# A one-layer hybrid decoder step: tokens in five tiles of 108 to 110 rows at both ends, the gate product on four row groups, the last block divided at 328 tokens

## What is computed

```python
xn = rmsnorm(x, norm_mix_g)
proj = xn @ w_in + b_in            # all branches' inputs and the gates
lg = log_sigmoid(ga @ w_gla_a2 + b_gla_a2) / 16      # ga: 16 columns of proj
...                                # three branches o_b: GLA, mLSTM, RG-LRU
x = x + (sum_b sigmoid(gates_b) * (o_b @ w_branch_b)) @ w_out
u = causal_dwconv(rmsnorm(x, norm_ffn_g) @ w_up)
x = x + (gelu(u_a) * u_b) @ w_down
y = rmsnorm(x, norm_f_g)           # y_prompt (512 rows), y_sample (32 rows)
```

## Time and profile before

| | us |
|---|---|
| median of three runs | 974.48 (974.48 to 976.2) |
| the profiled execution | 974.72 |
| its span, first to last instruction | 972.4 |
| TensorE busy | 955.5 (98%) |
| VectorE, ScalarE, GpSimd busy | 556.6, 427.0, 248.9 |

### The profile page before, as it was taken

The page is one execution under the profiler, slowest core; times in us unless marked ns, Lnnn a source line. Parts: engine busy times, 40 slices in busy tenths (PEclk is TensorE's granted clock), DMA queues, the critical chain, the costliest instruction groups (busy, mean ns, idle before and its releaser), DMA issues.

```text
span 972.4 us, 18988 instructions
## 1 busy us (share of the span) xinstructions
PE 955.5 (98%) x7595; PEld 938.0 (96%) x7595; DVE 556.6 (57%) x1002; ACT 427.0 (44%) x583; POOL 248.9 (26%) x130
## 2 busy tenths in 40 slices
PE   7999999999999999999999999999999999999997
PEld 6999999999999999899999999999999999999997
DVE  4494627899534445553236687777777777312122
ACT  5644434887345554223332355455455454212222
POOL 3543222333322323244342300000000002343340
PEclk9999999999999999999999999999999999999998
DMA  6335432243222124535224323332322221523212
GB/s 174 87 91 116 104 83 71 66 114 87 67 70 62 48 62 131 163 96 173 84 65 117 90 72 87 94 88 87 95 87 86 87 86 44 151 82 98 81 39 93
DMA packets 159983, 89.41 MB, mean 92 GB/s; under 512 B 6403, under 2 KB 158049, under 8 KB 159928
## 3 DMA queue, kind: packets, MB, share of 16 engines
q1 hardware_dynamic: 145024, 79.55, 29.1%
q10 hardware_dynamic: 14904, 9.07, 3.5%
HBM read 82.29 MB, written 6.32 MB: 91 GB/s over the span
## 4 chain that ended last, share of the span: by engine, by line
PE 94%; DVE 3%; ACT 1%; DMA 1%; issue 1%; ACTq 0%; DVEq 0%
PE ps L611 81%; PE ps L600 3%; PE ps L1076 2%; PE ps L827 1%; PE ps L619 1%; DMA xtok<-x_prompt 1%; PE ps L805 1%; DVE gv L1888 1%; PE ps L844 0%; PE ps L841 0%; PE ps L946 0%; PE ps L766 0%; PE ps L879 0%; PE ps L886 0%; PE ps L852 0%
## 5 line engine op out<-in xcount | busy, mean ns | idle before, releaser
L551 POOL TENSOR_TENSOR wlo<-stage,whi 128x1024 fp32r<-128x1024 f32 (+1 forms) x98 | 238.2, 2431 | 685.7 <-ACT whi L1166 685.5
L611 PE MATMUL ps<-xh,whi 128*128 128x272 f32 x1536 | 321.7, 291 | 0.0
L611 PE MATMUL ps<-xh,wlo 128*128 128x272 f32 x1536 | 317.7, 288 | 0.0
L611 PE MATMUL ps<-xl,whi 128*128 128x272 f32 x1536 | 316.9, 288 | 0.0
L611 PEld LDWEIGHTS ps<-xh,whi 128*128 128x128 f32 x1536 | 241.8, 188 | 3.1 <-issue 1.7
L611 PEld LDWEIGHTS ps<-xl,whi 128*128 128x128 f32 x1536 | 241.3, 188 | 0.0
L1166 ACT ACTIVATE whi<-stage 128x1024 fp32r<-128x1024 f32 x140 | 146.3, 1045 | 215.3 <-PE ps L611 209.0
L611 PEld LDWEIGHTS ps<-xh,wlo 128*128 128x128 f32 x1536 | 240.0, 189 | 0.0
L2166 DVE SCALAR_TENSOR_TENSOR ca<-up,par,ca 128x560 f32<-128x560 f32 x88 | 74.1, 842 | 7.6 <-DVE ca L2166 2.7
L611 PE MATMUL ps<-hh,whi 128*128 128x272 f32 x308 | 64.4, 291 | 0.0
L611 PE MATMUL ps<-hl,whi 128*128 128x272 f32 x308 | 63.6, 287 | 0.0
(11 more groups left out here) (466 smaller groups left out, 1347.4 us busy)
## 6 DMA issues: line engine op xcount, KB each, us to landing
stage<-w_in SPq DMA_DIRECT2D x52, 512.0 KB, 3.9
stage<-w_up SPq DMA_DIRECT2D x44, 512.0 KB, 3.8
stage<-w_down SPq DMA_DIRECT2D x16, 512.0 KB, 3.6
stage<-w_branch SPq DMA_DIRECT2D x12, 512.0 KB, 3.4
stage<-w_out SPq DMA_DIRECT2D x8, 512.0 KB, 3.6
stage<-w_down SPq DMA_DIRECT2D x8, 384.0 KB, 3.1
ch<-state_mlstm_C ACTq DMA_DIRECT2D x4, 512.0 KB, 5.2
s_mlstm_C<-ch ACTq DMA_DIRECT2D x4, 512.0 KB, 4.0
```

What stands on the lines that cost most here:

```text
L551: pool.tensor_tensor(wlo[:, slot, 0:kt], stage[:, slot, 0:kt], whi[:, slot, 0:kt].bitcast(F32), ALU.subtract).then_inc(s("lo"), 1)
L611: ins = mm(dst[:, r, :], w[:, slot, k0 + step * k, :], x(k)[:, r * HT:(r + 1) * HT], start=first and k == 0 and q == 0, stop=last and k == ...
```

## The change

Tokens form five tiles that all use most of the 128 rows: 0 to 110, 110 to 220, 220 to 328, 328 to 436, and the last 76 prompt tokens together with the 32 sample tokens. The tiles are loaded, scaled, transposed, transposed back and stored in these rows. The loads of the start go out without a wait between them, tiles 1, 3 and 2 on SP's queue, the two parts of tile 4 and tile 0 on ScalarE's; the norm takes the tiles in the order 4, 1, 0, 3, 2, the gain is copied after the first scaling, and the spare transposes are fewer and placed differently (24 and 4 at the front become 4 and 6; 6, 6, 6, 6, 9 between the real ones become 2, 12, 2, 4, 10). The load of unit 1 moves behind the small parameters. For the gate product, ga is written four times by half tokens at partitions 0, 32, 64 and 96, the weights likewise, and four matmuls stand on four row groups. In the residual stage ScalarE copies the odd blocks and VectorE the even ones, out of three PSUM pairs. The last block is divided at 328 tokens. ScalarE makes two stores at the end, the sample rows and the last 76 prompt rows.

The diff, without the places that only change row counts (`n = P if t < 4 else TS` becomes `n = tok_rows(t)`), semaphore counts and names:

```diff
-XN_ORDER = (4, 0, 1, 2, 3)
+XN_ORDER = (4, 1, 0, 3, 2)
+TOK = (0, 110, 220, 328, 436, T)
+TOK_P = SEQ - TOK[4]
+XN_OFF = 512 - TOK[4]
+XN_SPARE = (2, 12, 2, 4, 10)
+GAIN_C = 448
+XT_PAIR = (2, 3, 1)
 KT_DOWN = (8, 8, 6)
-CUT = 3 * P
+CUT = TOK[3]
...
+def tok_rows(t):
+
+    return TOK[t + 1] - TOK[t]
...
-        wa2 = at("wa2", [RANK, 2 * P], o + 4384)
+        wa2 = at("wa2", [P, P], o + 4384)
...
-        ga = at("ga", [RANK, T], o + 21216)
+        ga = at("ga", [P, HT], o + 21216)
...
-            for t in (1, 3):
-                sp.dma_start(xtok[:, t, :], io["x_prompt"][0, t * P:(t + 1) * P, :]).then_inc(s(f"tokens{t}"), 16)
+            def prompt_rows(t):
+                sp.dma_start(xtok[0:tok_rows(t), t, :], io["x_prompt"][0, TOK[t]:TOK[t + 1], :]).then_inc(s(f"tokens{t}"), 16)
+
+            prompt_rows(1)
+            prompt_rows(3)
             sp.dma_start(graw[:], io["norm_mix_g"].rearrange("l (r c) -> (l r) c", c=P)).then_inc(s("gain_in"), 16)
-
+            prompt_rows(2)
...
-            sp.wait_ge(s("tokens3"), 16)
-            load(1, one(qkv, 0), KT)
...
-            sp.dma_start(wa2[:], io["w_gla_a2"][0]).then_inc(s("bsmall_in"), 16)
+            for g in range(4):
+                sp.dma_start(wa2[32 * g:32 * g + RANK, :], io["w_gla_a2"][0, :, (g // 2) * P:(g // 2 + 1) * P])\
+                    .then_inc(s("bsmall_in"), 16)
             sp.dma_start(m0s, io["state_mlstm_m"].rearrange("l b h -> h (l b)")).then_inc(s("bsmall_in"), 16)
+            load(1, one(qkv, 0), KT)
...
-                    sp.dma_start(xp2[:], io["x_prompt"][0].rearrange("(t p) d -> p t d", p=P)).then_inc(s("late_in"), 16)
-                    sp.dma_start(xs2[:], io["x_sample"].rearrange("b t d -> (b t) d")).then_inc(s("late_in"), 16)
+                    for t in range(4):
+                        sp.dma_start(xp2[0:tok_rows(t), t, :], io["x_prompt"][0, TOK[t]:TOK[t + 1], :]).then_inc(s("late_in"), 16)
+                    sp.dma_start(xs2[0:TOK_P, :], io["x_prompt"][0, TOK[4]:SEQ, :]).then_inc(s("late_in"), 16)
+                    sp.dma_start(xs2[TOK_P:TOK_P + TS, :], io["x_sample"].rearrange("b t d -> (b t) d")).then_inc(s("late_in"), 16)
...
-                sp.dma_start(io["y_prompt"][0, t * P:(t + 1) * P, :], ytok[:, t, :]).then_inc(s("yout"), 16)
+                sp.dma_start(io["y_prompt"][0, TOK[t]:TOK[t + 1], :], ytok[0:tok_rows(t), t, :]).then_inc(s("yout"), 16)
...
-                awake(24, 5)
+                awake(4, 5)
                 pe.wait_ge(s("gain_in"), 16)
-                tr(bank(7)[:, 0:KD], graw[:], KD).then_inc(s("par_tr"), 1)
+                tr(bank(7)[:, GAIN_C:GAIN_C + KD], graw[:], KD).then_inc(s("par_tr"), 1)
...
+                awake(6, 5)
                 pe.wait_ge(s("gain"), 1)
                 for i, t in enumerate(XN_ORDER):
                     pe.wait_ge(s("xn"), i + 1)
                     for j in range(4):
                         if j == 3:
-                            awake(6 if i < 4 else 9, 7)
+                            awake(XN_SPARE[i], 7)
...
+                for g in range(4):
+                    q = slice(32 * g, 32 * g + RANK)
+                    ins = mm(bank(4 + g)[:, 0:HT], wa2[q, :], ga[q, :], start=True, stop=True)
...
-                if j >= 2:
-                    pe.wait_ge(s("xt"), j - 1)
-                for t in range(4):
-                    tr(pair(2 + j % 2)[:, t * P:(t + 1) * P], xp2[:, t, j * P:(j + 1) * P], P)
-                tr(pair(2 + j % 2)[:, SEQ:T], xs2[:, j * P:(j + 1) * P], TS).then_inc(s("xt_tr"), 1)
-
+                if j >= 3:
+                    pe.wait_ge(s("xt" if (j - 3) % 2 == 0 else "xt_odd"), (j - 3) // 2 + 1)
+                for t in range(5):
+                    n = tok_rows(t)
+                    src = xp2[0:n, t, j * P:(j + 1) * P] if t < 4 else xs2[0:n, j * P:(j + 1) * P]
+                    ins = tr(pair(XT_PAIR[j % 3])[:, XN_OFF + TOK[t]:XN_OFF + TOK[t + 1]], src, n)
+                ins.then_inc(s("xt_tr"), 1)
...
+            pe.wait_ge(s("xt"), 2)
+            pe.wait_ge(s("xt_odd"), 3)
...
-                    ins = tr(pair(2 + r)[0:n, shift + t * P:shift + (t + 1) * P], yb[:, r, t * P:t * P + n], P)
+                    ins = tr(pair(2 + r)[0:tok_rows(t), shift + t * P:shift + (t + 1) * P], yb[:, r, TOK[t]:TOK[t + 1]], P)
...
-            early_tiles, late_tiles = range(CUT // P), range(CUT // P, 5)
+            early_tiles, late_tiles = range(3), range(3, 5)
...
-            act.dma_start(xtok[0:TS, 4, :], io["x_sample"].rearrange("b t d -> (b t) d")).then_inc(s("tokens4"), 16)
-            for t in (0, 2):
-                act.dma_start(xtok[:, t, :], io["x_prompt"][0, t * P:(t + 1) * P, :]).then_inc(s(f"tokens{t}"), 16)
+            act.dma_start(xtok[TOK_P:TOK_P + TS, 4, :], io["x_sample"].rearrange("b t d -> (b t) d"))\
+                .then_inc(s("tokens4"), 16)
+            act.dma_start(xtok[0:TOK_P, 4, :], io["x_prompt"][0, TOK[4]:SEQ, :]).then_inc(s("tokens4"), 16)
+            act.dma_start(xtok[0:TOK[1], 0, :], io["x_prompt"][0, 0:TOK[1], :]).then_inc(s("tokens0"), 16)
...
             squares(4)
             root(4)
+            root(1)
             squares(0)
             root(0)
-            root(1)
+            root(3)
             squares(2)
             root(2)
-            root(3)
             hi_small()
...
-                    func(split(ga[:]), src[0:RANK], ACT.Identity, bias=cst[0:RANK, 2:3])
+                    for g in range(4):
+                        func(ga[32 * g:32 * g + RANK, :], src[0:RANK, g % 2, :], ACT.Identity, bias=cst[0:RANK, 2:3])
...
+            for j in range(1, KD, 2):
+                act.wait_ge(s("xt_tr"), j + 1)
+                func(xt[:, j, :], pair(XT_PAIR[j % 3])[:, XN_OFF:XN_OFF + T], ACT.Copy).then_inc(s("xt_odd"), 1)
...
-            store(io["y_sample"].rearrange("b t d -> (b t) d"), ytok[0:TS, 4, :])
+            then(func(ytok[0:n, 4, :], ytok[0:n, 4, :], ACT.Copy, scale=fstat[0:n, 4:5]))
+            store(io["y_sample"].rearrange("b t d -> (b t) d"), ytok[TOK_P:n, 4, :])
+            store(io["y_prompt"][0, TOK[4]:SEQ, :], ytok[0:TOK_P, 4, :])
...
-            for t in XN_ORDER[:3]:
-                scaled(t)
+            scaled(4)
             dve.wait_ge(s("par_tr"), 1)
-            v.tensor_copy(par[:, P_G1:P_G1 + KD], bank(7)[:, 0:KD]).then_inc(s("gain"), 1)
+            v.tensor_copy(par[:, P_G1:P_G1 + KD], bank(7)[:, GAIN_C:GAIN_C + KD]).then_inc(s("gain"), 1)
+            scaled(1)
             squares(3)
-            for t in XN_ORDER[3:]:
+            for t in XN_ORDER[2:]:
...
-            for j in range(KD):
+            for j in range(0, KD, 2):
                 dve.wait_ge(s("xt_tr"), j + 1)
-                v.tensor_copy(xt[:, j, :], pair(2 + j % 2)[:, 0:T]).then_inc(s("xt"), 1)
+                v.tensor_copy(xt[:, j, :], pair(XT_PAIR[j % 3])[:, XN_OFF:XN_OFF + T]).then_inc(s("xt"), 1)
+            dve.wait_ge(s("xt_odd"), KD // 2)
...
-                v.tensor_tensor(ytok[:, 0:4, bass.ds(col, P)], src[:, 0:4 * P].rearrange("p (t c) -> p t c", t=4),
-                                gfb[:, bass.ds(col, P)].unsqueeze(1).broadcast_to([P, 4, P]), ALU.mult)
-                v.tensor_tensor(ytok[0:TS, 4, bass.ds(col, P)], src[0:TS, 4 * P:5 * P], gfb[0:TS, bass.ds(col, P)],
-                                ALU.mult).then_inc(s("y_gain"), 1)
+                for t0, t1 in ((0, 2), (2, 5)):
+                    n = tok_rows(t0)
+                    ins = v.tensor_tensor(ytok[0:n, t0:t1, bass.ds(col, P)],
+                                          src[0:n, t0 * P:t1 * P].rearrange("p (t c) -> p t c", c=P),
+                                          gfb[0:n, bass.ds(col, P)].unsqueeze(1).broadcast_to([n, t1 - t0, P]), ALU.mult)
+                ins.then_inc(s("y_gain"), 1)
...
-            v.tensor_tensor(ytok[:, 3, last], bank(7)[:, 0:P], gfb[:, last], ALU.mult)
-            v.tensor_tensor(ytok[0:TS, 4, last], bank(7)[0:TS, P:2 * P], gfb[0:TS, last], ALU.mult).then_inc(s("y_gain"), 1)
+            n = tok_rows(4)
+            v.tensor_tensor(ytok[0:n, 3:5, last], bank(7)[0:n, 0:2 * P].rearrange("p (t c) -> p t c", c=P),
+                            gfb[0:n, last].unsqueeze(1).broadcast_to([n, 2, P]), ALU.mult).then_inc(s("y_gain"), 1)
             dve.wait_ge(s("std"), 3)
-            v.reciprocal(fstat[:, 3:4], fstat[:, 3:4])
-            v.reciprocal(fstat[0:TS, 4:5], fstat[0:TS, 4:5]).then_inc(s("y_rstd"), 1)
+            v.reciprocal(fstat[0:n, 3:5], fstat[0:n, 3:5]).then_inc(s("y_rstd"), 1)
```

More of the change, by code:

```diff
@@ L685, in v_a2 @@
                 pe.wait_ge(s("evac"), 1)
[L686 removed]
+                pe.wait_ge(s("bsmall_in"), 16 * 8)
                 pe.wait_ge(s("par"), 2)
[L688 to L691 removed]
+                for g in range(4):
+                    q = slice(32 * g, 32 * g + RANK)
+                    ins = mm(bank(4 + g)[:, 0:HT], wa2[q, :], ga[q, :], start=True, stop=True)
                 ins.then_inc(s("a2"), 1)
@@ L1082, in token_sums @@
```

(10 more changed lines are left out.)

75 lines of the change are left out of this document (39 added, 36 removed).

## The result

The changed kernel takes 988.36 us (median of 4 runs, 986.66 to 989.08), the kernel before, measured beside it, 975.29 (974.48 to 976.2). The ratio is 1.0131, with a 95% interval of 1.0118 to 1.0144: slower by 1.3%, where the forecast was 973.2 in a range of 968.8 to 975.9. The profiled execution of the changed kernel took 988.13 us, its span 985.8, 13.4 more than the span before. Where a kernel fell into a much slower state once (one execution of the kernel before at 1571.74, one of e5_before_mid at 1523.54), the medians and ratios of this document leave that execution out.

A forecast was written before the change was run, and what follows sets the result against it. The prediction took TensorE's work, 94% of the chain that ended last, as the bound. Its terms, +2.0 - 1.0 - 1.35 - 2.3 - 1.45 + 2.8 = -1.3, gave 973.2 us on the median's scale, range 968.8 to 975.9.

The forecast's parts named there:

- start until the projection: Start: tile 4, its 76 rows on four DMA engines, is squared at 10.8, so the projection starts near 20.2: +2.0 us.
- the projection: Small projection: five near-equal tiles per column block transpose in 0.53 instead of 0.78 us, four times: -1.0 us.
- gate product: Gate product: passes on four row groups overlap, 0.65 us in all instead of 34.90 to 36.92: -1.35 us.
- residual stage: Residual transposes: with ScalarE sharing the copies, TensorE sets the pace, 4.25 us instead of 6.6: -2.3 us.
- last block: Last block: 66 matmuls shrink from 384 to 328 columns, 66 others grow from 160 to 216: -1.45 us.
- from the last copy to the end: Tail: ScalarE's second store, 76 rows on four engines, follows the 32-row store on the same queue: +2.8 us.
- 29 of them take 10.7 us now ... so it is issued near 16: Start, SP's small issues: unit 1's load, issued near 16, lands near 20; conversion at about 21 leaves it hidden by 1 us.
- 110 rows then ride on 11 engines, 108 on 12: Token transfers: rows are dealt evenly to the largest engine count up to 16 that divides them; 76 rows ride on 4.
- two signs of being wrong: Both ends: the 76 rows move like any other tile; projection: TensorE takes 1.4 us a step instead of 0.72.
- the rival of the slower clock: Projection: with fewer spare transposes TensorE begins at its lower clock, half the work at half speed costs 3.9: 977.1; chance 0.14.
- The rival of the spread rows: Both ends: the 76 rows spread over all engines, tile 4 lands at about 5.5, tail +0.7: 969.1; chance 0.18.
- The last rival: Gate product: the four row groups don't overlap, it stays at 2.0 us: 974.6, no change; chance 0.05.

The follow-up runs named there:

- e5_before_mid: The kernel before with only the gate product on four row groups and the residual stage changed, that stage in 112- and 96-row tiles: 972.05 us, ratio 0.9962.
- e2_load1_early: The changed kernel with unit 1's load put back ahead of the small issues, behind a wait for tile 3: 981.61 us, ratio 1.0059.
- e11_tail96: The changed kernel with the 110- and 108-row end stores sent as 96 rows and the rest: 986.89 us profiled, first store to end 12.4.
- e12_tail96_64: The changed kernel with e11_tail96's end stores and the 76-row store sent as 64 and 12: 985.5 us profiled, first store to end 10.2.
- the cuts of the kernel before: The kernel before, four 128-row end stores each cut in two; first store to end 7.7 us whole, 8.2 (column halves) to 18.7 (76 + 52).
- e9_after_128_awake: The changed kernel with 128-row tiles, unit 1's load ahead of the small issues and 24 spare transposes ahead of the gain: 972.24 us, ratio 0.9976.
- this pair of runs: The changed kernel with 128-row tiles and unit 1's load early, with 4 or 24 spare transposes ahead of the gain: ratios 0.9985 and 0.9976.

## Why the prediction was wrong

| step | forecast, us | changed kernel, us |
|---|---|---|
| start until the projection | +2.0 | +5.5 (18.18 to 23.68) |
| the projection | -1.0 | +5.1: -1.0 of work, +4.4 stop (4.15 of it idle), +1.7 lower clock |
| gate product | -1.35 | -1.3 |
| the wait at 254 | not counted | +1.8 (9.2 late before it, 11.0 behind it), most of it the lower clock of this execution |
| residual stage | -2.3 | -2.5 |
| last block | -1.45 | -1.6, with the tail's shorter chain |
| from the last copy to the end | +2.8 | +6.5 |
| sum (of the exact terms) | -1.3 | +13.4 |

**What held.** The terms of the middle: five transposes between the projection's steps without the idle 0.17 (25.12 to 25.58), whose projection without a stop takes 9.5 us in e2_load1_early against 10.5 before; the gate product; the residual stage; 0.150 a matmul in the last block. The run with the gate product and the residual stage alone confirms these two on the whole time. The 76 rows do ride on four engines.

**The step that failed first: "29 of them take 10.7 us now ... so it is issued near 16".** I took SP's issues at their durations of before. But there most of them come when the token loads have flowed off. Behind loads that flow at 247 GB/s, the issue of one small load and the six of b_in, 3.5 us before, took 13.3 (in e11_tail96 and e12_tail96_64, with the same start, the small load took 7.2 instead of 5.67), and the load of unit 1 went out at 25.85, 10 us later than forecast. My 1 us of cover became a stop of 4.15, and behind the stop came the lower clock. e2_load1_early takes the load out from behind these issues: 6.7 us of the 13.1 between the medians. I had the issue in the working ("hidden by 1 us") and no case in the range in which SP itself is slowed. (The change puts 32 issues ahead of the load, not the 33 of the working; nothing hangs on that.)

**The step mis-sized at both ends: the price of uneven rows.** I counted the 76 rows only, and let the others go at full flow ("110 rows then ride on 11 engines, 108 on 12" stood there, without a price). At the end the four lowest engines carry 19 rows of the 76, and 38 of the 110- and 108-row stores ahead of them where they carried 32, and the whole flow drops, as the cuts of the kernel before show: +2.8 became +6.5. At the start the same: tile 4 at 13.50 instead of 10.8. Of the two signs of being wrong that the prediction names, the first (76 rows like any other tile) did not come: the mechanism was there, only its price was not. The second came, but late: a step of the projection takes 1.4 us behind the stop (32.42 to 33.85), where the rival of the slower clock has it from the projection's beginning. The rival of the spread rows ("dealt to all 16 engines") was wrong for a second reason: 112-row tiles, spread over all 16, still flow at 267 GB/s.

**The rival of the slower clock** had half of the truth. It said 977.1 from the removed spare transposes, and I gave it 0.14; e9_after_128_awake shows that with 128-row tiles they are worth 1.3 us of start. My argument against it ("some 50 transposes ... fill the 6 us") held for the projection, whose first step takes 0.77 as before (23.68 to 24.45; 18.18 to 18.95), but it left out that the transposes ahead of it go at half pace themselves. What that costs in the changed kernel, where tile 4 comes late, was not tried. The larger share of the lower clock came from the stop in the projection (0.51 from 32.4 to 37), which no rival had. Against the rule of the Trainium skill ("TensorE: Matmul & The Clock Gate", section "Part 4: PE-mode transpose") that transposes don't raise the clock, this pair of runs speaks as the rows of before did: with 20 more of them the pace has doubled when the real ones come, with nothing but transposes before, though the column of the granted clock reads 1.00 in both.

**The last rival** (the four row groups don't overlap) is out: 0.74 us.

So the tiles at both ends and the place of unit 1's load made the kernel slower; the fewer spare transposes did so at 128-row tiles. The gate product, the residual stage and the new order of the norm are gains, and together, with 128-row tiles at both ends, 24 spare transposes and the load in its old place, they make 970.44. The last block's other division was not tried alone.

## What to carry to other kernels

Before tokens are cut into tiles for the sake of TensorE, look at how each tile loads and stores: a transfer over all 128 partitions flowed half as fast again as one of 112 rows, and a row count without a large divisor up to 16 piles its rows on a few DMA engines (76 rows on four of 16). A DMA issue has no fixed price: behind a queue that flows slowly the same small load took 5.67 us instead of 1.10, and everything behind it on that queue is late. Try each part of a change alone, since gains of 1 to 3 us that held here were hidden under 17 us of loss at the two ends.

## What the runs showed of the hardware that was not expected

DMA engines that are all busy can still move a third less: share 1.04 at 267 GB/s against 1.02 at 406, by the row counts of the transfers alone.

The wait near 242 us is followed by the lower clock in some executions and not in others, with the same code and the same length. The kernel before (first fence) and the one with stores of 112 + 16 (second), which differ only after 960 us, both waited 2.4 us there:

```profile
242.00:244.40 2.40, 0.05 (x2) 0.04 (x1) 2.40 (x2) 1.66 (x2) 0.62 (x1) 1.00 0.44 153
244.40:249.00 4.60, 4.60 (x37) 4.51 (x38) 4.49 (x4) 0.59 (x1) 2.16 (x1) 1.00 0.23 55
```

```profile
242.00:244.50 2.50, 0.22 (x2) 0.00 (x1) 2.47 (x3) 1.66 (x2) 0.50 (x1) 1.00 0.51 179
244.50:249.00 4.50, 4.42 (x23) 4.42 (x24) 4.39 (x5) 0.00 (x0) 2.25 (x1) 0.62 0.18 38
```

From there on the second is 1.7 us later than the first; the runs of the kernel before lie near 974.5 or near 976.1, about as far apart. In the profiled execution of the changed kernel the wait was 2.6 and the clock fell; in e11_tail96 and e12_tail96_64, which differ from it only in the stores at the end, the wait was 2.6 too and the 24 matmuls behind it took 3.29. So this part of the time is the execution's luck and not the change's. What tips it was not tried.
